# Writing the heads of a gated recurrent layer token-major instead of channel-major, with the head norm as a free-axis sum

## The reference

```python
h = rms_norm_3(x, norm_g)
q, f_f, f_b, i, z = split_cols(h @ w_in, ODD_SPLITS)     # 2048 columns each
q = jax.nn.silu(q)
...
# hgrn2_direction, per chunk of 64 tokens:
#   o_t = (masked q k^T) v  +  q_t^T S      S: (128 x 128) state ahead of the chunk
#   S   = diag(decay) S + k_end^T v
o = o_f + o_b                                            # forward and backward
o = o * lax.rsqrt(jnp.mean(o * o, axis=-1, keepdims=True) + EPS)   # per head and token
o = o.reshape(B, S, HGRN_WIDTH) * head_norm_g
return (o * jax.nn.silu(z)) @ w_out
```

## Time and profile before

| what | value |
|---|---|
| median of 3 executions | 3370.01 us (3360.65 to 3373.13) |
| the profiled execution | 3364.78 us, its span 3363.0 us |
| TensorE matmul busy | 3145.2 us (94%), 16462 instructions |
| VectorE busy | 1504.5 us (45%), 2407 instructions |
| ScalarE busy | 704.5 us (21%), 1108 instructions |
| mean DMA rate | 175 GB/s |
| granted TensorE clock, mean | 0.983 |
| the odd layer | from 2579.98 us (first matmul) to the end at 3363 us |

### The profile page before, as it was taken

How to read it: one execution, slowest core, us unless ns; L and a number is a source line. 1 busy time by engine, 2 the same in 40 slices (tenths; PEclk the granted TensorE clock), 3 DMA queues, 4 the chain that set the end, 5 groups by cost and what they waited for, 6 DMA issues and landing times. The chain is left out here.

```text
span 3363.0 us, 39565 instructions
## 1 busy us (share of the span) xinstructions
PE 3145.2 (94%) x16462; PEld 1799.1 (53%) x16462; DVE 1504.5 (45%) x2407; ACT 704.5 (21%) x1108; POOL 0.2 (0%) x4
## 2 busy tenths in 40 slices
PE   7999999899998899999988988999999999999998
PEld 3476545444445433332322322788555887887875
DVE  2654247613857422222222121645444757476663
ACT  2210232403028100000000000100521333240513
POOL 0000000000000000000000000000000000000000
PEclk9999999999999999999999999999999999999999
DMA  7301044222022489999999999222211212221210
GB/s 271 126 2 52 26 148 159 88 88 99 16 71 74 176 343 427 428 428 427 428 428 428 427 428 422 84 84 85 71 55 55 76 51 76 76 76 51 76 51 26
DMA packets 120306, 588.36 MB, mean 175 GB/s; under 512 B 8896, under 2 KB 11072, under 8 KB 95424
## 3 DMA queue, kind: packets, MB, share of 16 engines
q1 hardware_dynamic: 120128, 585.83, 43.6%
HBM read 583.72 MB, written 2.10 MB: 174 GB/s over the span
## 5 line engine op out<-in xcount | busy, mean ns | idle before, releaser
L476 PE MATMUL ps<-hT,weight_ring 128*128 128x512 f32 x1216 | 537.3, 599 | 8.2 <-PEq L831 4.1
L476 PE MATMUL ps<-work,weight_ring 128*128 128x512 f32 (+1 forms) x944 | 407.5, 584 | 9.0 <-PEq L404 8.0
L476 PEld LDWEIGHTS ps<-hT,weight_ring 128*128 128x128 f32 x1216 | 230.4, 192 | 291.3 <-issue 289.0
L476 PEld LDWEIGHTS ps<-work,weight_ring 128*128 128x128 f32 x944 | 176.1, 191 | 200.2 <-issue 194.4
L333 DVE TENSOR_TENSOR work<-work,ps 128x512 f32<-128x512 f32 x196 | 134.7, 687 | 234.6 <-PE ps L463 229.7
L2425 PE MATMUL ps<-weight_ring,work 128*64 128x512 f32 x928 | 211.1, 597 | 27.3 <-DMA weight_ring<-in_w_up 18.7
L463 PE MATMUL ps<-weight_ring 128*128 128x256 f32 x896 | 202.8, 379 | 0.0
L2558 DVE SCALAR_TENSOR_TENSOR xT<-ps,mod,xT 128x512 f32<-128x512 f32 x128 | 96.1, 751 | 226.5 <-PE ps L2443 224.1
L463 PEld LDWEIGHTS ps<-weight_ring 128*128 128x128 f32 x896 | 169.6, 190 | 24.9 <-issue 1.9
L463 PE MATMUL ps<-hT,weight_ring 128*128 128x256 f32 x704 | 164.2, 390 | 7.7 <-PEq L404 3.9
L463 PE MATMUL ps<-weight_ring,spare_slot 128*128 128x256 f32 x704 | 159.6, 380 | 1.3 <-DVE weight_ring L294 1.3
(11 more groups left out here) (436 smaller groups left out, 4008.3 us busy)
## 6 DMA issues: line engine op xcount, KB each, us to landing
weight_ring<-in_w_up SPq DMA_DIRECT2D x31, 2048.0 KB, 38.6
weight_ring<-in_w_down SPq DMA_DIRECT2D x28, 2048.0 KB, 40.3
weight_ring<-in_w_gate SPq DMA_DIRECT2D x27, 2048.0 KB, 40.3
work<-in_w_down SPq DMA_DIRECT2D x26, 2048.0 KB, 40.3
work<-in_w_gate SPq DMA_DIRECT2D x21, 2048.0 KB, 40.3
weight_ring<-in_w_in_odd SPq DMA_DIRECT2D x20, 2048.0 KB, 7.7
weight_ring<-in_w_in SPq DMA_DIRECT2D x17, 2048.0 KB, 8.6
work<-in_w_up SPq DMA_DIRECT2D x17, 2048.0 KB, 36.9
```

What stands on the lines that cost most here:

```text
L476: ins = pe.matmul(bank[0:m, 0:f], w[:, k, where:where + m], src[:, k, 0:ntok], start=k == 0, stop=k == kt - 1)
```

## The change

The roles of the operands in `output(h)` are swapped. A head comes out token-major: partition = token within a block of 128, free axis = 4 blocks x 128 channels.

- The 4 intra-chunk matmuls have `aT` stationary and the values moving.
- The 14 inter-chunk matmuls have 64 query columns of one chunk stationary, and the 128 x 128 state moving. An even chunk writes partitions 0 to 63, an odd one 64 to 127, and even and odd chunks are issued in turn.
- The squares are summed along the free axis: four ScalarE activations of 128 x 128 per head with `accum_out` (`head_squares`). The root then is taken of 128 x 4 values (two heads in the tail: 128 x 8).
- `finish` and the tail's `scale` multiply with a root that is broadcast along the free axis (`head_scaled`).
- Each head is turned back to channel-major by four TensorE transposes (`turn`), all of them in the next block. The gate reads them out of PSUM banks 5, 6, 7 and 3.
- The table is moved: `root(0)` and `root(1)` stand at once behind `square(0)` and `square(1)` (tZ + 2, tZ + 3), `finish(0)` and `finish(1)` one tile earlier (tZ + 3, tZ + 4), the matmuls of ones are gone. In the tail, `turn(0)` and `turn(1)` stand ahead of the first tile, `turn(2)` and `turn(3)` behind tile 1. In the last projection `turn(2)` and `turn(3)` stand between the second and the third begun tile.

```diff
 def output(h): part(pe):
             for s in range(4):
-                pe.matmul(ps[:, bank, s * P:(s + 1) * P], I[:, s, h * P:(h + 1) * P], aT[h % 2][:, s, :],
+                pe.matmul(ps[:, bank, s * P:(s + 1) * P], aT[h % 2][:, s, :], I[:, s, h * P:(h + 1) * P],
                           start=s == 0, stop=False, skip_group_check=True)
-            for c in range(8):
-                cols = slice(c * 64, (c + 1) * 64)
-                for d in range(2):
-                    if (c > 0) if d == 0 else (c < 7):
-                        ins = pe.matmul(ps[:, bank, cols], state(d, c)[:, h, :], qd[d][:, h, cols], start=False,
-                                        stop=c == 7, skip_group_check=True)
+            even = [(0, 2), (0, 4), (0, 6), (1, 0), (1, 2), (1, 4), (1, 6)]
+            odd = [(0, 1), (0, 3), (0, 5), (0, 7), (1, 1), (1, 3), (1, 5)]
+            for n, pair in enumerate(zip(even, odd)):
+                for d, c in pair:
+                    rows, s = slice(64 * (c % 2), 64 * (c % 2) + 64), c // 2
+                    ins = pe.matmul(ps[rows, bank, s * P:(s + 1) * P], qd[d][:, h, c * 64:(c + 1) * 64],
+                                    state(d, c)[:, h, :], start=False, stop=n == 6, skip_group_check=True)
...
+def head_squares(ch, a, act, h, done):
+    sums, squares = head_roots(ch)[0], ch.slot(5)
+    for s in range(4):
+        a(act.activation(squares[:, h, s * P:(s + 1) * P], ch.ps[:, 3 + h % 2, s * P:(s + 1) * P], ACT.Square,
+                         accum_out=sums[:, 4 * h + s:4 * h + s + 1]), done if s == 3 else None)
+
+def head_scaled(ch, v, dve, h, done):
+    root = head_roots(ch)[1][:, 4 * h:4 * h + 4].unsqueeze(2).to_broadcast([P, 4, P])
+    out, got = (x.rearrange("p (s v) -> p s v", v=P) for x in (ch.slot(8)[:, h, :], ch.ps[:, 3 + h % 2, :]))
+    v(dve.tensor_tensor(out, got, root, MUL), done)
...
 def odd_tail(ch, G):
+    def turn(h):
+        def part(pe):
+            if h >= 2:
+                pe.wait_ge(scaled.sem, scaled.at(h - 1))
+            for s in range(4):
+                cols = slice(s * P, (s + 1) * P)
+                ins = pe.transpose(ps[:, banks[h], cols], natural[:, h, cols], ch.m("ident"))
...
     def gate(h):
         def part(v, dve):
-            t = roots[:, h, :]
-            if h >= 2:
-                v.after(rooted, h - 1)
-                v(dve.tensor_tensor(t, ps[:, 3 + h % 2, :], t, MUL))
-            v(dve.scalar_tensor_tensor(Z[:, h, :], t, ch.v("hgrn_head_norm_g_3", 4 * G + h), Z[:, h, :], MUL, MUL), complete)
+            v.after(turned, h + 1)
+            v(dve.scalar_tensor_tensor(Z[:, h, :], ps[:, banks[h], :], ch.v("hgrn_head_norm_g_3", 4 * G + h), Z[:, h, :],
+                                       MUL, MUL), complete)
...
-                        (tZ + 4, gram(3)), (tZ + 4, norm_sum(0)), (tZ + 5, norm_sum(1)), (tZ + 5, output(2)),
-                        (tZ + 6, output(3))):
+                        (tZ + 4, gram(3)), (tZ + 5, output(2)), (tZ + 6, output(3))):
...
+        beside.add(-1, seq(turn_last(0), turn_last(1)), roots_last, seq(scale_last(2), scale_last(3), gate_last(0)))
+        beside.add(1, seq(turn_last(2), turn_last(3)), None, gate_last(1))
+        beside.add(2, None, None, gate_last(2))
+        beside.add(3, None, None, gate_last(3))
```

More of the change, by code:

```diff
@@ L415, in _ @@
             if split:
-                count, half_ready, rest_ready = split
+                count, half_ready, between = split
                 ch.block_wait(pe, first)
@@ L423, in _ @@
                                   start=k == 0, stop=False)
-                rest_ready(pe)
+                    between.get(n, nothing)(pe)
             for n, t in enumerate(tiles):
@@ L2823, in odd_tail @@
 def odd_tail(ch, G):
[L2826 to L2829, removed]
+    ps, Z, natural = ch.ps, ch.slot(4), ch.slot(8)
+    rooted, scaled, turned, complete = ch.counters("tail_rooted", "tail_scaled", "tail_turned", "tail_heads_done")
+    sums, roots = (x[:, 8:16] for x in head_roots(ch))
+    banks = (5, 6, 7, 3)
     def square(a, act):
-        a(act.square(squares[:, 3, :], ps[:, 4, :]), squared)
@@ L2834, in add_up @@
[L2834 to L2839, removed]
-    def root(a, act):
[L2842 to L2846, removed]
+        head_squares(ch, a, act, 3, None)
@@ new lines, in root, with scale, part @@
+    def root(a, act):
+        inverse_root(a, act, roots, sums, 1.0 / P, ch.eps[:, 0:1], rooted)
+    def scale(h):
+        def part(v, dve):
+            v.after(rooted, 1)
+            head_scaled(ch, v, dve, h, scaled)
+        return part
+    def turn(h):
[5 more added lines that the diff above has]
+                ins = pe.transpose(ps[:, banks[h], cols], natural[:, h, cols], ch.m("ident"))
+            ins.then_inc(turned.sem, 1)
+            turned.total += 1
+        return part
@@ L2860, in heads @@
         return wait
-    return square, add_up, root, gate, heads
+    return seq(square, root), scale, turn, gate, heads
 def odd_group(ch, G, norm):
@@ L3044, in part @@
             a.after(summed, h + 1)
-            a(act.square(qd[0][:, h, :], ps[:, 3 + h % 2, :]), squared)
+            head_squares(ch, a, act, h, None)
         return part
@@ L3049, in part @@
         def part(a, act):
-            a.after(sums, h + 1)
-            inverse_root(a, act, qd[1][:, h, :], ps[:, 7, :], 1.0 / P, ch.eps[:, 0:1], rooted)
+            sums, roots = (x[:, 4 * h:4 * h + 4] for x in head_roots(ch))
+            inverse_root(a, act, roots, sums, 1.0 / P, ch.eps[:, 0:1], rooted)
         return part
@@ L3137, in odd_group @@
     for where, part in ((tB, log(0)), (tB + 2, exponents(0)), (tI, log(1)), (tI + 2, to_natural(0)), (tI + 3, exponents(1)),
-                        (chain[0] - 1, to_natural(1)), (tZ + 2, square(0)), (tZ + 3, square(1)), (tZ + 4, root(0)),
-                        (tZ + 5, root(1)), (tZ + 6, square(2))):
+                        (chain[0] - 1, to_natural(1)), (tZ + 2, square(0)), (tZ + 2, root(0)),
+                        (tZ + 3, square(1)), (tZ + 3, root(1)), (tZ + 6, square(2))):
         beside.add(where, scalar=part)
@@ L3167, in odd_layer @@
         odd_group(ch, G, norm if G == 0 else None)
-    square, add_up, root, gate, heads = odd_tail(ch, 3)
+    roots, scale, turn, gate, heads = odd_tail(ch, 3)
     return add_to_stream(ch, ch.slot(4), 8, 1, Norm(
         ch, ch.xT, ch.xT, T, [ch.v("final_norm_g_3", i) for i in range(8)], None, 7, ch.slot(0), ch.slot(1)),
-        {-1: seq(*[gate(h) for h in range(4)])}, seq(square, root), tensor_first=add_up, order=[0, 1, 2, 6, 3, 4, 5],
-        split=(4, heads(2), heads(4)))
+        {-1: seq(gate(0), gate(1), scale(2), scale(3), gate(2), gate(3))}, roots, tensor_first=seq(turn(0), turn(1)),
+        order=[0, 1, 2, 6, 3, 4, 5], split=(4, heads(2), {1: seq(turn(2), turn(3)), 3: heads(4)}))
 def block3(ch, norm):
```

29 lines of the change are left out of this document (9 added, 20 removed).

## The result

The changed kernel takes 3337.57 us (median of four executions, 3334.61 to 3340.36); the kernel before, run beside it, 3369.03 us (3360.65 to 3373.13). The ratio is 0.9908, 95% interval 0.9892 to 0.9925: faster by 0.9%. Run again later with five executions it took 3337.14 us, ratio 0.9914 (0.9898 to 0.9929).

A forecast was written before the change was run, and what follows sets the result against it. TensorE's own work bounds the kernel; 15.4 + 10.0 + 2.6 - 0.1 - 0.7 = 27.2 us saved gives 3337.6 us off the profiled execution, 3342.8 off the median; forecast 3339, range 3323 to 3356.

The forecast's parts named there:

- outputs of heads 0 to 2: Twelve outputs on TensorE's path: 14 state products each fall from 3.08 to 1.80 us, 15.4 us saved (12.2 to 18.5).
- matmuls of ones and their wait: In each group two matmuls of ones and a 0.69 us wait for ScalarE's root go: 2.49 us each, 10.0 saved.
- output(3) to the next block: At the four block ends ScalarE's squares are last, 4.03 us to the next block: 2.6 us saved.
- ordinary tails: In three blocks 16 transposes (1.74 us) replace two matmuls of ones (1.71 us): 0.1 us lost.
- last projection: In the last projection a 1.00 us wait goes and 0.4 + 0.9 + 0.4 come in: 0.7 us lost.
- The rival without overlap: State products' halves don't run side by side, 0.110 us a record; only 9.2 us gained, 3355.6 or 3358 us; chance 0.10.
- the slower one: Every change of half in the state products costs 0.13 us, nothing overlaps: 20 us slower, 3385 us; chance 0.03.
- the square: At a block's end, one 128 x 128 ScalarE square with accumulator reading and hand-over takes 0.48 us, four 1.92.
- My 5 us for a block end that TensorE alone sets: Saving from output(3) to the next block if TensorE alone, needing 2.69 us, set the end: 5 us.
- the first gates at 2.2 us: In the last projection turn(0) ends after 0.5 us, then two gates of 0.77 us each: 2.2 us.
- The wait of 0.4 us that I forecast at turn(2) or turn(3): In the last projection two begun tiles end at 5.65 us, but head 3 is scaled only at 6.5 us.
- The rival with a longer switch: Each of a root's two table switches costs a second load's time (1.28 us): 4.4 us, so 3343 us; chance 0.02.

The follow-up runs named there:

- the run with the halves in runs: Changed kernel with an output's 14 state products issued as seven of one half, then seven of the other: 3349.5 us, ratio 0.9959.
- two runs on head 2: Changed kernel with head 2's four squares done twice (layer 10.7 us longer), and with them moved ahead of the last Silu (3334.93 us, ratio 0.9902).
- the run on heads 0 and 1: Changed kernel with the four squares of heads 0 and 1 done twice: 753.8 us for the odd layer, against 754.3 in the changed kernel.
- early transposes, twice: Changed kernel with heads 0 and 1 transposed behind output(3), before the barrier: layer 753.7 us; also with head 2's squares ahead of the last Silu: 3336.75 us.
- squares twice: Changed kernel with the four squares of head 2 done twice: the layer grew by 10.7 us.

## Why the prediction was right

Forecast were 27.2 us off the profiled execution and 3339 us; the stretches show 28.8, the median 3337.6. The saving is what the prediction can be held to. That 3339 lies within 1.4 us of the median is partly luck: the executions spread over 6 us, and the two medians are 31.5 us apart where the stretches show 28.8. By its steps:

| term | forecast | measured |
|---|---|---|
| outputs of heads 0 to 2 | 12 x 1.28 = 15.4 | 12 x 1.26 = 15.1 |
| matmuls of ones and their wait | 4 x 2.49 = 10.0 | 4 x 2.65 = 10.6 |
| output(3) to the next block | 2.6 | 0.66 + 1.00 + 1.00 + 0.69 = 3.35 |
| ordinary tails | -0.1 | 0.0 |
| last projection | -0.7 | -0.4 |
| sum | 27.2 | 28.7 (the stretches: 28.8) |

- **The products.** Right in mechanism and size: 1.67 us against my 1.80, and 0.15 us on the neighbours, as I read it for the change of mode. The rival without overlap fell with the first profile, the slower one with it, and the run with the halves in runs shows that overlap is the cause. The shorter load is not: the new shape, 64 columns loaded and 128 moved, with each half in a run, brings 0.110 down to 0.101 us a record only, and the halves side by side bring it to 0.060. The 28 loads would take 1.5 us by the figure of the Trainium skill, TensorE: Matmul & The Clock Gate, section LDWEIGHTS, which is an estimate. With the halves in runs the products take 2.82 us, so the time of the loads isn't what they go by there. With the halves side by side they take 1.67, near that estimate (the timeline's row of the 28 loads is 1.51 us long), and no run shows whether the loads set that time.
- **The matmuls of ones.** From gram(3) to output(2) 5.24 us now (3098.55 - 3093.31), of which 3.46 is the tile. Before it was 7.89 (3115.97 - 3108.08), so 2.65 are gone:

```profile
3108.08 1.95 PE L2986 MATMUL ps<-work 128*128 128x128 f32 x16
...
3110.72 3.62 PE L463 MATMUL ps<-weight_ring 128*128 128x256 f32 x16
```

My 2.49 was too small since I took the idle time of 0.69 that the row shows for the cost of the wait. That cost is a difference of starts, like the others: 3115.03 - 3110.72 - 3.46 = 0.85. Leaving the sums out of the kernel before gives the same 2.7 us per group, so this term is of its own, whatever becomes of the products.

- **ScalarE at the block's end.** The step was right, and two runs on head 2 show it from both sides (1.59 us more with more squares, 0.69 less with the squares moved). Mis-sized was the square: 0.40 us from one to the next, not 0.48, because the reading of the accumulator begins 0.17 us after an activation of 0.28 started. ScalarE's end came at 3.29 us in place of 3.57, and the term was 0.7 us too small. The first of the four block ends took 4.10 us instead of 3.76, for a cause that stays open (see the run on heads 0 and 1). My 5 us for a block end that TensorE alone sets was too small as well: with the squares of head 2 moved it is 3 x 1.69 + 1.38 = 6.45.
- **The tails.** From the start of a block to gram(0) of its group pass 145.38 us before and 145.37 changed (3273.58 - 3128.20, 3253.90 - 3108.53). The transposes cost 0.06 us more than the two sums, and the first tile 0.07 less behind them.
- **The last projection.** Half right. I had the first gates at 2.2 us and they were at 2.35: that wait is there, with 1.29 us. The wait of 0.4 us that I forecast at turn(2) or turn(3), and named as a sign, isn't: head 3 was scaled at 6.21 us in place of 6.5, for the same reason as above, and TensorE came 0.2 us later than I thought. The term is 0.3 us smaller by it.
- **Table switches.** The rival with a longer switch fell. The load begins 0.02 us after the last reading of the accumulator, and the logarithm starts 1.30 us after its table load began:

```profile
3265.14 0.19 ACT L2832 ACTIVATION_READ_ACCUMULATOR work<-ps 128x1 f32 x1
3265.35 1.28 ACT L588 ACT_TABLE_LOAD   x1
3266.65 0.30 ACT L588 ACTIVATE small<-small,eps 128x4 f32<-128x4 f32 x1
```

The 1.38 us of drain that the Trainium skill, ScalarE: Activation LUTs, section What ACT_TABLE_LOAD costs, adds to each switch are not there; the measurement decides.

## What to carry to other kernels

If a product has a short moving side (64 columns) and a full stationary one, swapping the two and letting the results fall on the two halves of the output partitions nearly halves its time (here 3.08 to 1.67 us for 14 products), provided both halves are fed within a few instructions of each other. Token-major results also turn a sum over partitions into a free-axis sum on an engine with room, and the transposes back cost half of the matmuls of ones that they replace (0.9 us for two heads against 1.71). After such a gain ask at each barrier which engine is now the last: here ScalarE was, and one line that moves its squares into an idle stretch gave 3.1 us more in the stretches, which whole executions could not tell from nothing.

## What the hardware showed beyond what I expected

- An idle stretch of TensorE can cost more than its own length. After gaps of 1.98 us (early transposes, twice) and 2.61 us (squares twice) the granted clock fell to the lower level for a while, and the work behind took 1.4 to 1.7 us more. Filling the gap with useless transposes kept it at 1.00. But the length doesn't decide alone: the kernel without transposes has a gap of 2.70 us ahead of its begun tiles, and the clock stays at 1.00 there. One of the four ends with the doubled squares was spared too, and at another the fall came only behind the following gap of 1.29 us, a gap that the changed kernel has too (there the clock is 1.00 all the way from 3287 to 3298 us). What else decides stays open.
- Two neighbouring products on the same half cost nothing (1.68 us for 28 records in either order), seven in a row cost 1.15 us.
- A root of 128 x 4 values takes 0.30 and 0.20 us, but its two table loads 2.56: the small shape hardly shortens the chain that the change moved.
